# Large SBUF buffers of a fused encoder layer moved to starts that are multiples of 512 bytes

## The reference

```python
h = x + rmsnorm(token_mixer(rmsnorm(x, g1), w_in, ..., w_out), g2)
y = h + rmsnorm(conv_ffn(rmsnorm(h, g3), w_up, cw, cb, w_down), g4)

def token_mixer(xn, ...):
    proj = xn @ w_in                      # 2048 x 7184
    # 8 stick-breaking attention heads, 8 gated-DeltaNet heads (chunks in the reference of 64 tokens)
    mix = concat([o_sb, o_dn]);  return mix @ w_out      # 2048 x 2048

def conv_ffn(xn, w_up, cw, cb, w_down):
    h = causal_dwconv(xn @ w_up, cw) + cb                # 2048 x 11264, width 3
    gate, val = split(h);  return (gelu(gate) * val) @ w_down   # 5632 x 2048
```

## The kernel before

| buffer | start before | mod 512 | mod 64 |
|---|---|---|---|
| `xfeat` (`res`) | 192 | 192 | 0 |
| `raw` | 16576 | 192 | 0 |
| `w_hi` | 49344 | 192 | 0 |
| `w_lo` | 65728 | 192 | 0 |
| `half` | 82112 | 192 | 0 |
| `ident`, `ones` | 86208, 86720 | 192 | 0 |
| `token_scale` | 89360 | 272 | 16 |
| `xhl` (`down`) | 91456 | 320 | 0 |
| `arena` (`act`, `mix`) | 124224 | 320 | 0 |

## Time and profile before

### The profile page before, as it was taken

How to read it: one execution, slowest core, us unless ns; L and a number is a source line. 1 busy time by engine, 2 the same in 40 slices (tenths; PEclk the granted TensorE clock), 3 DMA queues, 4 the chain that set the end, 5 groups by cost and what they waited for, 6 DMA issues and landing times.

```text
span 1292.0 us, 20357 instructions
## 1 busy us (share of the span) xinstructions
PE 1248.0 (97%) x6681; PEld 1071.6 (83%) x6681; DVE 887.6 (69%) x1625; ACT 735.9 (57%) x1448; POOL 218.8 (17%) x258
## 2 busy tenths in 40 slices
PE   7997999999999999899999999999999999999996
PEld 6886889889877788788888888888888888888885
DVE  6677886685434655588878878887887874555543
ACT  5675645754577645575566566556656554444442
POOL 1111140223012000013122222322222220000000
PEclk9898999999999999899999999999999999999998
DMA  9364533463333555345555455455545565555541
GB/s 380 125 219 127 178 131 125 142 215 109 133 128 130 176 187 192 131 165 193 195 194 185 174 194 195 167 190 195 195 173 194 185 228 196 187 179 189 194 163 65
DMA packets 33029, 226.82 MB, mean 176 GB/s; under 512 B 4160, under 2 KB 4816, under 8 KB 6352
## 3 DMA queue, kind: packets, MB, share of 16 engines
q1 hardware_dynamic: 30528, 218.12, 47.5%
q10 hardware_dynamic: 2448, 8.00, 1.8%
HBM read 223.86 MB, written 2.24 MB: 175 GB/s over the span
## 4 chain that ended last, share of the span: by engine, by line
PE 88%; DVE 5%; ACT 4%; issue 1%; DMA 1%; POOL 0%; ACTq 0%; DVEq 0%; POOLq 0%
PE bank L1292 33%; PE bank L1294 17%; PE bank L1310 10%; PE bank L1308 10%; PE bank L1309 10%; DVE w_lo L860 2%; DVE arena L881 1%; PE bank L1401 1%; ACT w_hi L437 1%; PE bank L1377 1%; PE bank L1394 1%; PE bank L1392 1%; PE bank L1361 0%; PE bank L1339 0%; DMA base_rows<-arena 0%
## 5 line engine op out<-in xcount | busy, mean ns | idle before, releaser
L860 DVE TENSOR_TENSOR w_lo<-raw,w_hi 128x512 fp32r<-128x512 f32 x816 | 572.8, 724 | 285.7 <-ACT w_hi L437 283.9
L1292 PE MATMUL bank<-xhl,w_hi 128*128 128x512 f32 x2048 | 731.4, 398 | 10.3 <-DVE w_lo L860 9.4
L437 ACT ACTIVATE w_hi<-raw 128x512 fp32r<-128x512 f32 x816 | 502.6, 631 | 376.2 <-PE bank L1310 189.8
L1294 PE MATMUL bank<-xhl,w_lo 128*128 128x256 f32 x2048 | 581.2, 284 | 0.0
L1292 PEld LDWEIGHTS bank<-xhl,w_hi 128*128 128x128 f32 x2048 | 387.9, 189 | 99.1 <-DVE xhl L903 9.4
L1294 PEld LDWEIGHTS bank<-xhl,w_lo 128*128 128x128 f32 x2048 | 388.2, 190 | 0.0
L1310 PE MATMUL bank<-w_hi,ffn_act 128*128 128x512 f32 x352 | 138.9, 395 | 0.0
L1308 PE MATMUL bank<-w_hi,ffn_act 128*128 128x512 f32 x352 | 138.9, 395 | 0.0
L1309 PE MATMUL bank<-w_lo,ffn_act 128*128 128x512 f32 x352 | 138.9, 395 | 0.0
L409 POOL TENSOR_TENSOR arena<-arena,token_scale 128x256 f32<-128x256 f32 x88 | 78.0, 900 | 308.1 <-DVE arena L865 192.7
L1214 DVE SCALAR_TENSOR_TENSOR arena<-arena,fcw 128x256 f32<-128x256 f32 x176 | 85.3, 485 | 23.9 <-DVE arena L1214 1.5
(11 more groups left out here) (217 smaller groups left out, 1006.2 us busy)
## 6 DMA issues: line engine op xcount, KB each, us to landing
raw<-in_wts SPq DMA_DIRECT2D x204, 1024.0 KB, 4.7
xfeat<-in_x SPq DMA_DIRECT2D x4, 512.0 KB, 9.2
xfeat<-in_x_tok ACTq DMA_DIRECT2D x1, 2048.0 KB, 12.6
arena<-base_rows ACTq DMA_DIRECT2D x4, 512.0 KB
out_y<-xfeat SPq DMA_DIRECT2D x4, 512.0 KB, 2.9
arena<-gate_rows ACTq DMA_DIRECT2D x1, 1024.0 KB, 4.7
arena<-in_post_gains ACTq DMA_DIRECT2D x1, 1024.0 KB, 4.8
down_gain<-in_post_gains ACTq DMA_DIRECT2D x1, 1024.0 KB, 4.7
```

The lines of the kernel that those rows point to most:

```text
L437: nc.scalar.activation(w_hi[:, i % RING, :], raw[:, slot, quarter * PIECE:(quarter + 1) * PIECE], ACT.Copy).then_inc(hi_ready, 1)
L860: V.tensor_tensor(w_lo[:, i % RING, :], raw[:, slot, quarter * PIECE:(quarter + 1) * PIECE], w_hi[:, i % RING, :].bitcast(f32), ALU.subtra ...
L1292: M(ps[j][:, :], w_hi[:, r % RING, w], xhl[:, k, :, :].rearrange("p a t -> p (a t)"), start=(k == 0), stop=False, skip_group_check=True)
L1294: last = M(ps[j][:, 0:T], w_lo[:, r % RING, w], xhl[:, k, 0, :], start=False, stop=(k == KT - 1), skip_group_check=True)
```

## The change

The small buffers and `half` are allocated first. A padding buffer (56 fp32 values) then fills up to the next multiple of 512 bytes, and `xfeat`, `raw`, `w_hi` and `w_lo` follow. Their sizes are multiples of 512 bytes, so `xhl` and `arena` behind them begin at such multiples too.

```diff
-        xfeat = sb("xfeat", [P, KT, T])
-        res = xfeat[:, :, :].rearrange("p k t -> p (k t)").rearrange("p (j d) -> p j d", j=NJ)
-        raw = sb("raw", [P, RAW, CHUNK])
-        w_hi = sb("w_hi", [P, RING, PIECE], f32r)
-        w_lo = sb("w_lo", [P, RING, PIECE], f32r)
         half = sb("half", [P, 4, T])
         ident = sb("ident", [P, P])
         ones = sb("ones", [P, P])
...
         mark = sb("mark", [P, 4])
         token_scale = sb("token_scale", [P, 2, T])
+        line = 512
+        pad = sb("pad", [P, (-nc.sbuf_base) % line // 4])
+        xfeat = sb("xfeat", [P, KT, T])
+        res = xfeat[:, :, :].rearrange("p k t -> p (k t)").rearrange("p (j d) -> p j d", j=NJ)
+        raw = sb("raw", [P, RAW, CHUNK])
+        w_hi = sb("w_hi", [P, RING, PIECE], f32r)
+        w_lo = sb("w_lo", [P, RING, PIECE], f32r)
```

## The result

The changed kernel is faster. Its median is 1287.72 us (1276.37 to 1292.61, nine runs) against 1296.26 us (1293.84 to 1299.41, nine runs): ratio 0.9916, 95% interval 0.9895 to 0.9938. (The ratios here are estimated from all runs of both kernels; they aren't the quotients of the medians, which would be 0.9934.) The forecast was 1295.4 us and no change. Its executions also lie much further apart (16 us) than those of the kernel before (6 us).

The account below looks back on a forecast made before the run. TensorE was taken to bound the kernel, with VectorE and ScalarE counting before 540 us. All terms were 0: 1293.84 + 0 = 1293.84 us, plus 1.56 us to the median, 1295.4 us; range 1291.0 to 1299.5.

Parts of the forecast that it names:

- The likeliest case: Whole kernel: only addresses differ, all costs taken at 0, no change at 1295.4 us; chance 0.78.
- What bounds the kernel: From 540 us to the end only TensorE's own pace matters much; before that, VectorE and ScalarE count too.
- VectorE, ScalarE, GpSimd, DMA at 0: Element-wise instructions, hold-ups and transfers keep their durations: 0, bounds 1.2 us (VectorE, ScalarE) and 2.1 us (first transfer).
- my estimate was 0.1 us: First transfer of xfeat: starting at a multiple of 256 bytes would take 0.1 us off, sum 1295.3.
- a clash between the streamed operand and the weights: TensorE streams: equal address bits of both operands don't disturb each other, since short load bursts take 0.97 and 0.98 us; 0.
- how a matmul starts: Start of each of 6681 TensorE matmuls: alignment taken to change nothing, 0, bounds -34 and +34 us.
- 5.1 ns fixed: Part of each TensorE matmul left beside 0.443 ns per column, if 512- and 256-column forms share one slope.
- already streams at the same slope from 192 and from 320: Argument against faster matmul starts: moving operands at two different offsets modulo 512 already show the same slope.
- weights clash with the moving operand: Slower rival, 256-column matmuls of the tile blocks: loads 10% slower at equal low bits, +12 us, 1307; chance 0.07.
- matmuls start sooner: Faster rival, all 6681 matmuls: 1 of 5.1 fixed ns saved by aligned starts, 6.7 us, 1288.7; chance 0.05.
- 34 us either way: Bounds on TensorE's matmul starts: whole fixed part of 6681 matmuls gone, or doubled.

Follow-up runs that it names:

- the sweep: TensorE's streams alone, nothing of the layer computed: bursts of 48 matmuls at chosen address differences modulo 256; 226.7 to 234.3 ns per 512-column matmul.
- the kernel with 192: Changed kernel with all large buffers beginning at 192 modulo 512, distance from w_hi to xhl kept at 32768 bytes: 1287.97 us, ratio to before 0.9933.
- A layout with one settled step: Changed kernel padded so that modulo 256 xhl is at 0, w_hi 128, w_lo 64, arena 128: 1283.93 us, ratio to before 0.9913.
- the untraced one of 1277.63 us: One execution of the changed kernel padded to xhl 0, w_hi 192, w_lo 0, arena 192 modulo 256; median of that kernel 1293.21 us.

## Why the prediction was wrong

The likeliest case (0.78) was no change at 1295.4 us, from 1291.0 to 1299.5; 1287.72 lies outside.

- **What bounds the kernel**: right. All that changed is TensorE's pace, in the two stages where it has no idle time.
- **VectorE, ScalarE, GpSimd, DMA at 0**: right, by the rows above. The first transfer went from 4.16 to 4.11 us. By the Trainium skill (DMA: Bandwidth & Descriptors, How a descriptor splits into AXI transactions) my estimate was 0.1 us, worked out for runs of 8192 bytes; this transfer has 4096 bytes in each partition, for which the same count is 134 beats in place of 128, an estimate of 0.2 us. The trace has less than either.
- **TensorE, a clash between the streamed operand and the weights, taken at 0 from L1427 and L1377**: the step that failed. The resource was the right one, the row was not. Those are 128-column matmuls that start every 111 to 113 ns; at the 0.443 ns per column of a 226.7 ns matmul the moving read needs only 57 of them, so a stall in it can hide. Where 512 columns move, the same two differences, 0 and 64, give 226.7 and 233.3 ns. The change of the difference from 128 to 0 was worth 5.7 ns in each of 1056 down matmuls, 6.0 us, and 4.4 in each of 1344 tile blocks of the traced execution, 5.9 us.
- **TensorE, how a matmul starts, taken at 0**: the split into 0.443 ns per column and 5.1 ns fixed was no property of a matmul. It rested on equal slopes in both forms, and the starts show 232.4 ns for 512 columns in the token form, but 230.6 and 120.6 ns for the two matmuls of the tile form. (The counts 914 and 777 also take in matmuls that only overlap an end: by starts, 350.1 is 351.2 and 231.7 is 232.4.) After the change the token form takes 226.7 ns, which is 0.443 per column with nothing left over, and the 340.0 ns blocks of the sweep (227.0 and 113.0) have the same 0.443; so in the token form what I called fixed was the stall. The argument that the engine "already streams at the same slope from 192 and from 320" was empty too. Those were not two cases but one: `w_hi` at 192 with `act` at 320, and `xhl` at 320 with `w_hi` at 192, both have a difference of 128 modulo 256.
- **Rival "weights clash with the moving operand"** (0.07, 1307): right in place, wrong in sign. Equal low bits are the quick case for 512 columns; it was the kernel before that paid. In the tile form the sign depends on the execution: 353.4 ns against 351.2 is +2.2 ns, 346.8 is -4.4. The Trainium skill (SBUF — State Buffer, Who interferes with whom), cited there, calls TensorE's two read ports independent. The sweep doesn't agree: with no other engine at work, the same matmuls take 226.7 or 233.3 ns by the difference of the two addresses.
- **Rival "matmuls start sooner"** (0.05, 1288.7): nearest in time by luck, not in mechanism. Starts at multiples of 512 don't set the step: the kernel with 192 has the 226.7 ns, the changed kernel with 128 bytes more has lost them, with its rings still at such multiples.
- **The range**: it bounded TensorE's unknown at 34 us either way and then left both ends out. The distance between the two operands, of all quantities the one that the change altered, had one value in the whole trace of the two streams that matter; that should have kept a wide range.

## What to carry to other kernels

Where matmuls of reduced fp32 data run back to back and each loads its weights, the start of the weights less the start of the moving operand, modulo 256, sets the pace by up to 3% (226.7 to 234.3 ns for 512 columns, at 0 and at 96). It is free to choose with a few bytes of padding, and any change of layout can turn it, in either direction. Before a trace is taken as evidence that something doesn't matter, check that it holds two values of the quantity, and that the row is bound by the resource in question. A layout with one settled step (346.7 and 228.9 ns here) gives steadier times, at a ratio level with that of the changed kernel (0.9913 and 0.9916).

## What the runs showed of the hardware

- TensorE's pace depends on where its two operands start relative to each other, with no other engine at work. Token form, 512 columns, settled: 226.7 ns at a difference of 0, 228.9 (at times 233.3) at 192, 232.3 at 128, 233.3 at 64, each modulo 256; a change of 32 bytes from 0 to 32 costs 6.6 ns.
- In the quickest steps seen, 226.7 ns for 512 columns and 340.0 for a tile block (227.0 and 113.0), the time is in proportion to the columns, 0.443 ns each at the full granted clock, with no fixed part left. The 346.7 ns of the changed kernel are 6.7 above that: 231.7 and 115.0.
- Some pairs have two settled steps (346.7 and 353.3 ns per tile block at 0 and 0; 340.0 and 350.0 at 192 and 0), taken after a stop of the stream and held, in the up projection for 466 or 475 us. What chooses between them stayed open, as did what in the memory has the period of 256 bytes.
- No traced execution held the 340.0 ns step through the up projection; the untraced one of 1277.63 us may have.
